# The attention branch as seven block products a unit, its rows added by transfers and by VectorE

## The reference, cut to what matters

```
branch_a = a @ w_attn_branch            # a: T x 1024, w: 1024 x 2048
branch_b = b_out @ w_conv_branch        # T x 1024, 1024 x 2048
merged = sigmoid(ga + b_gate[0]) * branch_a + sigmoid(gb + b_gate[1]) * branch_b
x = x + rmsnorm(merged @ w_o, g_mix_post)
```

## Time and profile before

| | us |
|---|---|
| median of 3 runs | 2650.47 (2649.92 to 2650.8) |
| span of the profiled execution | 2648.5 |
| conv units, 672 matmuls | 738.25 to 820.20 |
| attention branch, 768 matmuls | 820.20 to 911.95 |
| first unit of w_o, 112 matmuls | 911.95 to 936.50 |

### The profile page before, as it was taken

The page is one execution under the profiler, slowest core; times in us unless marked ns, Lnnn a source line. Parts: engine busy times, 40 slices in busy tenths (PEclk is TensorE's granted clock), DMA queues, the critical chain, the costliest instruction groups (busy, mean ns, idle before and its releaser), DMA issues.

```text
span 2648.5 us, 55450 instructions
## 1 busy us (share of the span) xinstructions
PE 2641.1 (100%) x20949; PEld 2582.9 (98%) x20949; DVE 2221.4 (84%) x3913; ACT 1386.6 (52%) x2533; POOL 189.5 (7%) x289
## 2 busy tenths in 40 slices
PE   9999999999999999999999999999999999999999
PEld 8999999999999999999999999999999999999899
DVE  7988888888896687898888888888888768789987
ACT  6544555555563255655555555555555453445454
POOL 0221000000010000000000000000000000000000
PEclk9999999999999999999999999999999999999999
DMA  6676334333484355655566555665569575565774
GB/s 229 187 209 184 134 117 142 133 124 117 158 262 160 131 165 158 247 174 161 169 206 186 181 162 167 191 198 175 158 188 306 158 239 173 162 207 162 251 265 151
DMA packets 160028, 479.65 MB, mean 181 GB/s; under 512 B 17177, under 2 KB 51361, under 8 KB 156480
## 3 DMA queue, kind: packets, MB, share of 16 engines
q1 hardware_dynamic: 128752, 370.81, 39.7%
q0 software_dynamic: 30960, 106.59, 18.0%
q10 hardware_dynamic: 144, 0.15, 0.0%
HBM read 420.63 MB, written 55.71 MB: 180 GB/s over the span
## 4 chain that ended last, share of the span: by engine, by line
PE 97%; DVE 2%; issue 0%; ACT 0%; DMA 0%; SPq 0%; DVEq 0%; ACTq 0%
PE pair L1208 78%; PE pair L1173 6%; PE pair L1328 3%; PE pair L1306 3%; PE pair L1111 2%; PE pair L935 1%; PE pair L1285 1%; PE pair L1133 1%; PE pair L987 1%; PE pair L1008 1%; DVE v_lo L1977 0%; DVE lo L2328 0%; PE pair L997 0%; DMA s_raw<-in_sstream 0%; PE pair L1068 0%
## 5 line engine op out<-in xcount | busy, mean ns | idle before, releaser
L1208 PE MATMUL pair<-o_hi,v_hi 128*128 128x260 f32 x5840 | 1657.6, 284 | 1.2 <-DVE v_lo L1977 0.8
L1208 PE MATMUL pair<-o_hi,v_lo 128*128 128x260 f32 x5840 | 1650.1, 283 | 0.0
L1404 ACT ACTIVATE v_hi<-s_raw 128x512 fp32r<-128x512 f32 (+1 forms) x1368 | 852.1, 626 | 931.3 <-PE pair L1208 795.3
L1208 PE MATMUL pair<-lo,v_hi 128*128 128x260 f32 x4172 | 1179.3, 283 | 0.0
L1977 DVE TENSOR_TENSOR v_lo<-s_raw,v_hi 128x512 fp32r<-128x512 f32 (+1 forms) x1288 | 874.0, 681 | 301.1 <-ACT v_hi L1404 265.1
L1208 PEld LDWEIGHTS pair<-o_hi,v_hi 128*128 128x128 f32 x5840 | 1099.0, 188 | 14.9 <-issue 11.9
L1208 PEld LDWEIGHTS pair<-o_hi,v_lo 128*128 128x128 f32 x5840 | 1100.8, 188 | 0.0
L1208 PEld LDWEIGHTS pair<-lo,v_hi 128*128 128x128 f32 x4172 | 784.8, 188 | 0.2
L1208 PE MATMUL pair<-lo_E,v_hi 128*128 128x260 f32 x834 | 236.2, 283 | 0.0
L1404 ACT ACTIVATE v_hi<-s_one 128x512 fp32r<-128x512 f32 (+1 forms) x220 | 137.1, 626 | 189.1 <-PE pair L1208 164.5
L1208 PE MATMUL pair<-lo_A,v_hi 128*128 128x260 f32 x834 | 235.3, 282 | 0.0
(11 more groups left out here) (287 smaller groups left out, 2494.7 us busy)
## 6 DMA issues: line engine op xcount, KB each, us to landing
s_raw<-in_sstream SPq DMA_DIRECT2D x468, 512.0 KB, 4.9
s_one<-in_sstream POOLq DMA_DIRECT2D x168, 512.0 KB, 5.4
raw<-f_scr SPq DMA_DIRECT2D x12, 1040.0 KB, 7.6
s_raw<-in_sstream SPq DMA_DIRECT2D x32, 384.0 KB, 4.0
g_scr<-d_h SPq DMA_DIRECT2D x16, 520.0 KB, 2.7
g_in<-g_scr SPq DMA_DIRECT2D x32, 260.0 KB, 2.8
x_scr<-y_sb SPq DMA_DIRECT2D x8, 1040.0 KB, 5.3
s_one<-in_sstream POOLq DMA_DIRECT2D x16, 384.0 KB, 4.8
```

The costliest lines, as they stand in the source:

```text
L1208: mm = pe.matmul(out, wt[:, slot, kk * P:kk * P + P], r[:, k, :], start=j in (0, 1, 3) and k == 0 and n == 0, stop=k == nk - 1 and n == 2, ...
L1404: nc.scalar.activation(v_hi[:, n % 4, 0:width], src, ACT.Copy, scale=0.5 if halved(u) else 1.0).then_inc(v_hi_rdy, 1)
```

## The change

The attention branch becomes eight units like the conv units (u = 40 to 47, `U_AT` = 40), so that `branch_unit` serves both, with `af_hi`, `af_lo` as operand: 8 x 84 = 672 matmuls in place of 768. What that brings with it:

- The attention steps run head pair by head pair (`step_of`). The output of a pair's four steps gathers in `aw`, DVE makes its forms (`attention_form`, four operations of 260 elements), and POOL stores them in `af_scr` with two transfers a pair; the last pair's forms are made in u = 33 and stored between the sums for u = 35 and 36. SP loads five forms in u = 34 (behind a wait for that store) and two in u = 39.
- Each unit's results go to one of four buffers `acc` and are gated there (`attention_gated`). Rows 0 to 7 are added to `x_tile` by POOL, by accumulating transfers from SBUF to SBUF (`add_row`), two in each of the sums for u = 43 to 46; each waits for the row before to have landed. Rows 8 to 15 are added by DVE (`merge`).
- `t1` of w_o's operand comes in u = 43 (rows 0 to 3, and of the other form half) and u = 45, each behind a wait for rows (`rows_merged`); s1, s3 and half of t2 in u = 47.
- The weights of the branch lie in pairs as those of the conv branch; its sum s1 is made by POOL as well (8 more sums of 2 x 256 KB). ACT's high parts for w_o's operand wait for the end of the stage.

```diff
+def step_of(n):
+    return n % 4, n // 4
...
             for u in range(U_BR, U_O):
+                if u == U_BR + 2:
+                    sp.wait_ge(af_stored, 32 * 4)
+                    af_load(0, 1, 2, 3, 4)
+                if u == U_AT - 1:
+                    for j in range(2):
+                        product_done(u, j)
+                        af_load(5 + j)
...
-                    for kk in range(4):
-                        k = 4 * h + kk
-                        for i, (wt, r) in enumerate(((v_hi, br_hi(k)), (v_hi, br_lo[:, k, :]),
-                                                     (v_lo, br_hi(k)))):
-                            for half in range(2):
-                                mm = pe.matmul(pair[2 + p][:, half, 0:HALF],
...
+                    if j == 6 and u >= U_AT:
+                        merge(2 * (u - U_AT))
+                    if U_BR + 3 <= u < U_AT and j == 6:
+                        af_low(u - U_BR - 3)
...
+                    if u == U_AT + 3 and j == 2:
+                        rows_merged(dve, KH // 2)
+                        t1(1, 0)
+                    if u == U_AT + 5 and j == 2:
+                        rows_merged(dve, KH)
+                        t1(1, 1)
...
                 pool.dma_start(s_one[:, c], sstream[r_of(u), 2, :, c]).then_inc(s1_dma, 16)
+                add_row(2 * (u - 3 - U_AT))
                 pool.wait_ge(s1_dma, 32 * summed(u) - 16)
                 pool.dma_start(s_one[:, c], sstream[r_of(u), 3, :, c], accum_op=ALU.add).then_inc(s1_dma, 16)
+                add_row(2 * (u - 3 - U_AT) + 1)
+
+            def add_row(m):
+
+                if not 0 <= m < BY_DMA:
+                    return
+                pool.wait_ge(br_free, KD + m + 1)
+                if m:
+                    pool.wait_ge(merged_in, 16 * m)
+                pool.dma_start(x_tile(m), two(acc[(U_AT + m // 2) % 4][:, m % 2, :]), accum_op=ALU.add)\
+                    .then_inc(merged_in, 16)
```

More of the change, by code:

```diff
@@ L223, in build @@
         pT_sb = sub("pT_sb", [P, 2, 4, BLK])
-        a_st = [sub(f"a_st{i}", [P, 2, BLK]) for i in range(2)]
+        aw = sub("aw", [P, 2, T])
         assert o[0] <= r_g + KD * XB
@@ L386, in build @@
         SPLIT += [(u, j, u % 2) for u in range(U_BR, U_O) for j in range(7)]
-        BR_S = len(SPLIT)
-        SPLIT += [("br", m, h) for m in range(KD) for h in range(2)]
         SPLIT += split_of(range(U_O, U_UP))
@@ L552, in build @@
         a_rdy = sem("a_rdy")
-        a_stored = [sem(f"a_stored{i}") for i in range(2)]
-        br_in = [sem(f"br_in{i}") for i in range(4)]
+        af_rdy = sem("af_rdy")
+        af_stored = sem("af_stored")
+        merged_in = sem("merged_in")
         br_hi_rdy = sem("br_hi_rdy")
@@ L683, in h_store, with af_load @@
                 sp.dma_start(dram, d_h[u % 2][:, :, :]).then_inc(h_stored[u % 2], 16)
-            def br_load():
-                for c in range(4):
-                    sp.dma_start(br_raw[:, 2 * c:2 * c + 2, :], a_scr[:, 2 * c:2 * c + 2, :])\
-                      .then_inc(br_in[c], 16)
+            def af_load(*forms):
+                for j in forms:
+                    sp.dma_start(af_raw[j][:, :, :], af_scr[CONV_FORM_AT[j], :, :, :]).then_inc(op_in[j], 16)
             def cf_load(*forms):
@@ L746, in _ @@
                     next_gate(2 * (u - 1 - U_BR) + 1)
-            next_gate(KD - 2)
-            next_gate(KD - 1)
-            for m in range(KD):
-                next_gate(KD + m)
-                if m % 4 == 3:
-                    load(R_BR + m // 4 + 2)
             PIECES = (("11", 0, 0), ("12", 0, 1), ("21", 1, 0), ("22", 1, 1))
@@ L1300, in conv_unit @@
                     n = s_of(u, j, u % 2)
-                    if u == U_BR:
-                        pe.wait_ge(br_rdy, j + 1)
+                    if u in (U_BR, U_AT):
+                        pe.wait_ge(br_rdy, j + (1 if u == U_BR else 8))
                     pe.wait_ge(v_lo_rdy, n + 1)
                     for k in range(KC):
-                        for i, (wt, r) in enumerate(((v_hi, cf_hi[j]), (v_hi, cf_lo[j]), (v_lo, cf_hi[j]))):
+                        for i, (wt, r) in enumerate(((v_hi, hi[j]), (v_hi, lo[j]), (v_lo, hi[j]))):
                             mm = pe.matmul(out, wt[:, n % 4, k * P:k * P + P], r[:, k, :],
@@ L1459, in o_high @@
                     if 3 <= s <= 5:
[L1460 removed]
+                        act.wait_ge(op_in[j], 16 * (s + (j < 4)))
+                    elif s == 1 and j in (0, 3, 5):
+                        rows_merged(act, 4 * h + (4 if j == 0 else KH + 4))
                     elif j in (1, 2, 4, 6):
@@ L2751, in conv_unit @@
                         s3(u + 1, 1 - h)
-                    if U_BR + 1 < u < U_O - 2 and j in (3, 5):
-                        br_low(rows_split(u) + j // 5)
-            def branch(m):
-                dve.wait_ge(v_used, BR_H + 2 * m + 2)
-                dve.wait_ge(g_rd[m % 4], 16 * (KD // 4 + m // 4 + 1))
-                row, g = x_tile(m), two(g_in[m % 4][:, :])
-                if m:
-                    dve.wait_ge(merged_ready, m)
-                dve.scalar_tensor_tensor(out=two(ma_sb[:, :]), in0=g, scalar=1.0, in1=both(2 + m % 2),
-                                         op0=ALU.add, op1=ALU.mult).then_inc(br_free, 1)
-                dve.wait_ge(br_free, KD + m + 1)
-                dve.tensor_tensor(row, row, two(ma_sb[:, :]), ALU.add).then_inc(merged_ready, 1)
@@ L3173, in _ @@
                     add_conv_sum(U_BR + 1)
-                pool.wait_ge(a_rdy, n + 1)
-                blk, w = n // 4, n % 4
-                pool.dma_start(a_scr[:, 2 * w:2 * w + 2, blk * BLK:(blk + 1) * BLK],
-                               a_st[n % 2][:, :, :]).then_inc(a_stored[n % 2], 16)
-            for u in range(U_BR + 2, U_O):
+                if n % 4 == 3:
+                    w = n // 4
+                    if w == 3:
+                        add_conv_sum(U_BR + 2)
+                        add_conv_sum(U_BR + 3)
+                    pool.wait_ge(af_rdy, 4 * w + 4)
+                    pool.dma_start(af_scr[0:4, :, w, :].rearrange("n p t -> p n t"),
+                                   aw.rearrange("p r (h t) -> p (r h) t", h=2)).then_inc(af_stored, 16)
+                    pool.dma_start(af_scr[4:7, :, w, :].rearrange("n p t -> p n t"),
+                                   (last_forms if w == 3 else cv_forms)[:, 0:3, :]).then_inc(af_stored, 16)
+            for u in range(U_BR + 4, U_O):
                 add_conv_sum(u)
```

286 lines of the change are left out of this document (159 added, 127 removed).

## The result

The changed kernel takes 2661.16 us (median of five runs, 2658.36 to 2663.8), the kernel before 2650.47: a ratio of 1.0039 with a 95% interval of 1.0028 to 1.0051. It is 10.7 us slower; forecast were 2642.7 us and "faster". Its profiled execution took 2659.18 us, with a span of 2657.4 us. The rows of the kernel before are named by their group; those of after follow, in the same order.

A forecast was written before the change was run, and what follows sets the result against it. PE was taken as the bound, busy 2641.1 of 2648.5 us. From the median 2650.5, minus 9.8 for matmuls, plus 0.5 and 1.5 for PE's stands at the two t1 halves, gave 2642.7 us; range 2640.0 to 2651.0.

The forecast's parts named there:

- The matmuls: Attention units: 672 matmuls instead of 768, at the conv stretch's price 81.96 us instead of 91.75, 9.8 us less.
- What a row costs: Row additions by POOL between the weight sums: 4.7 us to landing each, bounds 3.8 and 8.0.
- When row 3 goes out: POOL's queue before t1: row 3 issued at 852.8, landing at 857.5, or by 861 if weights hold it up.
- (d): Rival, slower: rows and sums hamper each other in every unit that has both, four units; 2658 us, chance 0.08.
- The wait at t1: First half of t1, u = 43: DVE waits 1.5 us for rows, mostly covered; PE stands 0.5 us.
- a cover of 2.3 to 2.7: Time in us by which DVE's results may come late before PE needs them; 2.3 counted for the tighter places.
- The forecast for A5: Second half of t1, u = 45, waiting for rows 4 to 7: DVE waits 3 us, PE 1.5 us.
- DVE in A0 to A7 and the sum chain: Units u = 40 to 47: DVE's work fits the unit within the cover, cost 0; weight sums drift 0.3 us in two units.
- 2.2 us of slack in the chain: Weight sums: the last conv unit's sum lands at 805.6, s2 starts at 807.85; up to 2 us may go to stores.
- The end of the stage: Start of w_o: s2 ends 6.9 us behind the stage's end, first half fits by 0.6 us; cost 0, at worst 0.5.
- (c): Rival: sum chain falls behind for good, or rows take over 6 us; 5 to 11 us come back, about 2648, chance 0.23.

The follow-up runs named there:

- experiment 9: Changed kernel, with SyncE asking for the weights of u = 41 and 43 only when row 0, or row 3, has landed: 2664.31 us, ratio 1.0058.
- experiment 3: Changed kernel, with the first half of t1 and its wait for four rows one unit later, in u = 44: 2664.08 us, ratio 1.005.
- experiment 4: Changed kernel, with rows 4 to 11 instead of 0 to 7 added by transfer: 2660.61 us, ratio 1.0041.
- experiment 1: Changed kernel, with all 16 rows added by VectorE and none by transfer: 2649.09 us, ratio 0.9996.
- experiment 2: Changed kernel, with rows 0 to 7 neither transferred nor added, so the output lacks their attention part: 2648.89 us, ratio 0.9994.
- experiment 12: As experiment 11, but forms 5 and 6 split at products 1 and 2 of u = 40 again: 2645.94 us, ratio 0.9985.
- experiment 11: On experiment 10: forms loaded and split one unit earlier, none split in u = 39, forms 5 and 6 at products 2 and 4 of u = 40: 2647.45 us.
- experiment 10: On experiment 1: s1 of the first w_o unit by two more transfers, first halves of t2 and t3 inside u = 47: 2648.06 us, ratio 0.9992.
- experiment 5: On experiment 1: eight transfers of the same source and size at the old places, into bytes nobody reads: 2652.35 us, ratio 1.0009.
- experiment 6: Changed kernel, with only rows 0 to 2 by transfer and the other 13 by VectorE: 2650.21 us, ratio 1.0003.

## Why the prediction was wrong, step by step

**The matmuls: right.** PE has 96 fewer, and wherever nothing waits, a group costs what the conv stretch costs: 21.86 us for 180 is 0.1214 each, 81.96 / 672 is 0.1220.

**What a row costs: the step that failed.** The prediction took 4.7 us with bounds of 3.8 and 8.0, from transfers of other kinds. In the changed kernel the median is 4.8. But the two rows on which most hung took 10.3 and 9.5, above the bound. The Trainium skill's estimate of 2.6 us (DMA: Bandwidth & Descriptors, Anatomy of one DMA) was farther off still; no row of this kernel took less than 3.8. I had seen the weights coming ("or by 861 if the weights of 793.33 + 61.5 = 854.8 hold it up") and gave them 3.5 us. A row that meets them lands in 9.3 to 11.2 us when it goes out 0.6 to 3.0 us behind them, in the changed kernel and in every experiment with real rows, and in 7.9 us when it goes out with them (experiment 9). That is 4 to 7 us more than the others.

**When row 3 goes out: failed too.** The timeline had it at 852.8; it was 861.58. Row 2 went out at 857.13, 9 us behind its place on my timeline. Half of this came before any row: the first step of the sum for A3 went out at 839.17, where my timeline, carried back to it, has 792.94 + 41.0 + 0.7 = 834.6. PE and SyncE were as late (the weights went out at 859.55 instead of 854.8), by the stands in C5 and A0. The other half is row 0, which held row 1 back for 10.3 us (839.77 to 850.1). I had let only a row's issue cost time in POOL's queue, and written of (d) "its data can move while a sum waits to be confirmed". In the code each row waits for the row before, and each sum stands behind a row in the queue; a late landing stops both.

**The wait at t1.** I had 1.5 us of wait in A3, nearly all under a cover of 2.3 to 2.7, and 0.5 us of PE. It was 9.1 us of wait and 9.6 of PE. The trace adds up to it: row 3 went out 8.8 us late (861.58 against 852.8) and took 4.8 us more to land (9.5 against 4.7), VectorE came 4.2 us late (862.0 against 857.8), and 0.3 us had been in hand: 9.1 us. PE stood from 864.1, and the rest of the row's lateness went through in full. The forecast for A5 (3 us of wait, 1.5 of PE) did not occur in the changed kernel, since everything behind A3 had been shifted by 11 us and rows 4 to 7 were then early; in experiments 3, 4 and 9, where A3 lost less or nothing, A5 waited 8.7, 9.35 and 5.1 us.

**The slow clock: missing.** No term or rival had it. It cost 1.9 us behind A3 and 1.7 around 835 us (18 and 38 matmuls in windows that were busy for 3.09 and 5.00 us, where 27 and 44 fit, at 8.8 per us).

**DVE in A0 to A7 and the sum chain: cost 0, in fact 4 to 9.** Even with no transfer of rows (experiments 1 and 2) PE stood at 790, 830, and 0.43 us at each t1. In their traces the stage ends at 910.86 and 908.82, 8.7 and 6.7 us behind the 902.2 that the matmuls alone would give; in the changed kernel 4.3 us are left for it. I had 2.2 us of slack in the chain and allowed "up to 2 us" of it for the stores and loads of forms. At the seam this slack was gone: at 789.66 VectorE had waited 2.5 us for s_one. In A0 I had counted two low parts; the trace has three splits of 1.24 us there (822.94, 827.11, 829.47), the first of them left over from C7, and VectorE had no cover left to lend. I had counted the chain and VectorE apart, each against the same 2.3 us of cover. Experiment 12 shows part of it: with forms loaded and split earlier the stand at 790 goes. The last 1.3 us at 830 are VectorE's row of work with two splits in it; no run shortened it at that place, and splitting form 6 later (experiment 11) made PE wait for that form itself.

**The end of the stage: "fits by 0.6 us", in fact 2.0 too late.** I counted from a VectorE that is idle at the stage's end, as before. It entered the w_o unit with two gates, two additions, and both halves of t2 and t3 ahead of s2. s2 ended 8.0 us behind the stage's end instead of 6.9. But the chain of waits shows that s2 was the smaller part: it held PE for 0.60 us. The rest came from all that stands behind s2 on VectorE, low parts up to y_sb at 940.28, which I had not followed. Experiment 10 takes 1.0 us of it back.

**The rivals.** What came is nearest to (d), which had 0.08: rows and sums hamper each other. Its mechanism, 3.6 us per unit in four units, is not what the trace shows: it was one wait of 9 us. The ingredients were in (c) ("or rows take over 6 us"), with a price of 5 to 11 us, of which the prediction said 2648. The sum of what was found is 9.5 (A3, 11.5 instead of 2.0), 4.3 (seam and C5, to the end at 917.99, less the 0.5 us by which the conv stretch began earlier) and 2.0 (w_o): 15.8 us, which stands for 944.54 against the 928.7 that the forecast would give. Of the 18.5 between forecast and median 2.7 are left, and they have no cause that the runs show: 0.9 lies behind 944.54, and the median of the runs is 2.0 above the profiled execution (0.2 too much, since 1.8 us of that execution lie outside its span, not 2.0).

## What to carry to other kernels

Before a transfer takes work from an engine, look for what that engine's work waits on: here DVE's eight additions were worth nothing that could be measured, and the transfer put a landing in front of it. Price a transfer not at the median of its kind but at what it takes when the largest periodic load on the chip is asked for beside it, and put that load's issue times on the same timeline; a serial queue then hands one late landing to all behind it, so moving the wait or the load only changes who waits. Where two stages are joined, count slack once: what the queue, the engine and the start of the next stage each leave free is the same few microseconds.

## What the hardware showed that I had not expected

- An accumulating transfer of 260 KB from SBUF to SBUF took 3.8 to 6.0 us to land in the changed kernel, but 9.5 to 10.3 us when 2 MB of loads by another engine were issued 1.4 to 2.0 us ahead of it; with these loads held back, row 3 took 4.8 us and the rows that then met them 7.9 to 11.1.
- The granted clock of PE fell to 0.50 (1.2 GHz) in a stand of 9.6 us and was 0.77 in the window that begins 1.3 us after PE has started again. After stands of 1.7 to 2.0 us in A0 it fell in some kernels (to 0.66 in the window behind in experiments 3 and 10; 0.79 and 0.87 in the changed kernel) and stayed at 1.00 in others (experiments 2, 4, 5 and 6).
